# Attention's division moved behind attention, and ten expert conversions moved with it, in a hybrid decoder layer on eight cores

## The reference, cut to what matters

```python
# branch A, for each of 16 heads of 64: three (window, dilation) patterns, merged by their softmax denominators
num = sum(w * o for w, o in zip(weights, outs))
y_att = merge_heads(num / sum(weights)) @ w_att
# branch B: retention in chunks of 128, 4 heads, per-head norm, silu gate
y_ret = (merge_heads(rmsnorm(retention(q, k, v), g_ret)) * silu(gr)) @ w_ret
# merge
x = x + (sigmoid(ga + ba) * y_att + sigmoid(gb + bb) * y_ret) @ w_out
# then x = x + experts(rmsnorm(x)): 32 experts, top-2 inside the top-1 group of 8
```

## Time and profile before

| | us |
|---|---|
| median of three runs (1596.06 to 1598.11) | 1596.18 |
| the profiled execution | 1601.79 |
| its span on the slowest core, core 1 | 1597.6 |
| spans of the eight cores | 1574.9 to 1597.6 |
| TensorE busy | 1370.9 (86%) |
| VectorE, ScalarE, GpSimd busy | 763.3, 695.2, 762.8 |
| moved by DMA | 267.03 MB |

### The profile page before, as it was taken

The page is one execution under the profiler, slowest core; times in us unless marked ns, Lnnn a source line. Parts: engine busy times, 40 slices in busy tenths (PEclk is TensorE's granted clock), DMA queues, the critical chain, the costliest instruction groups (busy, mean ns, idle before and its releaser), DMA issues.

```text
span 1597.6 us, 29878 instructions; the slowest of 8 cores (1574.9 to 1597.6 us)
## 1 busy us (share of the span) xinstructions
PE 1370.9 (86%) x10037; PEld 789.1 (49%) x10037; DVE 763.3 (48%) x1239; ACT 695.2 (44%) x1191; POOL 762.8 (48%) x874
## 2 busy tenths in 40 slices
PE   4899998888879999999999899999999736565675
PEld 2344547776744444444444444444445435454563
DVE  3787774766656556555656411111354652211122
ACT  3576668887853444434443411111233542222232
POOL 1379981333236657666756312221225645543453
PEclk9999999998999999999999999999999957887888
DMA  9747866786765769999994399875964785999985
GB/s 221 215 92 131 165 155 177 163 188 139 179 138 89 118 101 131 125 131 146 122 137 123 61 289 166 131 125 129 244 220 154 228 286 153 275 254 251 281 162 91
DMA packets 105502, 267.03 MB, mean 167 GB/s; under 512 B 43352, under 2 KB 65368, under 8 KB 98818
## 3 DMA queue, kind: packets, MB, share of 16 engines
q0 software_dynamic: 29280, 124.30, 49.7%
q1 hardware_dynamic: 76066, 140.76, 28.4%
HBM read 285.71 MB, written 116.65 MB: 252 GB/s over the span
## 4 chain that ended last, share of the span: by engine, by line
PE 69%; DMA 13%; DVE 5%; issue 4%; ACT 4%; POOL 2%; SPq 1%; another core or an unknown queue 0%; DVEq 0%; POOLq 0%; ACTq 0%
PE ps L169 69%; DMA arena<-xn,idx 8%; DMA zret<-arena 5%; DVE arena L169 4%; ACT arena L169 3%; POOL arena L169 2%; DMA cfs_sb<-cfs 1%; DVE arena L167 1%; SPq L169 1%; DMA vp<-arena 0%; DVEq L156 0%; DVE logit L169 0%; ACT L169 0%; POOLq L176 0%
## 5 line engine op out<-in xcount | busy, mean ns | idle before, releaser
L169 PE MATMUL ps<-arena 128*128 128x512 bf16 (+5 forms) x8208 | 1275.5, 313 | 78.5 <-ACT arena L169 32.5
L169 PEld LDWEIGHTS ps<-arena 128*128 128x128 bf16 (+1 forms) x8208 | 679.0, 102 | 587.1 <-issue 122.4
L169 ACT ACTIVATE arena<-ps 128x512 bf16<-128x512 f32 (+5 forms) x600 | 422.5, 719 | 450.6 <-PE ps L169 412.2
L169 POOL TENSOR_TENSOR arena<-arena 128x512 bf16<-128x512 f32 (+4 forms) x274 | 347.7, 1278 | 297.9 <-DVE arena L169 244.7
L169 DVE TENSOR_TENSOR arena<-ps,arena 128x512 f32<-128x512 f32 (+4 forms) x420 | 235.3, 572 | 347.0 <-ACT arena L169 159.8
L169 PE MATMUL ps<-cbs_sb,arena 128*128 128x128 bf16 x1408 | 131.1, 232 | 107.3 <-DMA arena<-xn,idx 69.7
L169 DVE SCALAR_TENSOR_TENSOR arena<-arena,ps 128x512 f32<-128x512 f32 x176 | 115.5, 683 | 192.3 <-PE ps L169 190.7
L169 PEld LDWEIGHTS ps<-cbs_sb,arena 128*128 128x128 bf16 x1408 | 100.7, 104 | 176.2 <-issue 147.8
L169 ACT ACTIVATE arena<-arena 128x8 f32<-128x8 f32 (+5 forms) x225 | 148.6, 665 | 59.0 <-DVE arena L169 29.1
L169 DVE TENSOR_TENSOR arena<-arena 128x1024 bf16<-128x1024 bf16 (+9 forms) x176 | 130.7, 750 | 75.7 <-ACT arena L169 68.7
L169 POOL DMA_INDIRECT out<-arena,idx x48 | 76.3, 1590 | 126.5 <-ACT arena L169 66.6
(11 more groups left out here) (60 smaller groups left out, 339.9 us busy)
## 6 DMA issues: line engine op xcount, KB each, us to landing
wb<-wexp POOLq DMA_DIRECT2D x60, 768.0 KB, 13.8
arena<-wb SPq DMA_DIRECT2D x30, 1536.0 KB, 15.4
arena<-x SPq DMA_DIRECT2D x32, 512.0 KB, 7.8
arena<-vx POOLq DMA_DIRECT2D x12, 768.0 KB, 5.1
arena<-wri POOLq DMA_DIRECT2D x8, 1024.0 KB, 23.1
zret<-arena SPq DMA_DIRECT2D x16, 512.0 KB, 19.8
arena<-zret SPq DMA_DIRECT2D x4, 2048.0 KB, 17.2
out<-arena SPq DMA_DIRECT2D x16, 512.0 KB, 9.8
```

Of the source, the lines that this page charges most:

```text
L169: ins = getattr(engobj, meth)(*a, **kw)
```

## The change

Five edits, made together:

1. **The division leaves attention.** `den_shift`, `den_act` and `z_out` are gone. After its last copy each head stores its numerators (64 rows of 2048 float32) and one row of denominators to DRAM (`head_out`). In step 1 of retention one VectorE reciprocal works on all 16 x 2048 denominators as a 128x256 tile (`den_rec`), which goes back to DRAM.
2. **The division is done in 32 pieces of 128x512**, one for each pair and group c. `div_load` loads numerators (128 rows of 2 KB) and the reciprocals spread over 64 partitions for each of the two heads (128 rows of 2 KB), and `div_mul` multiplies on VectorE into `za[c]`. Groups 0 and 1 are done in steps 51 to 61 of retention with four buffers, groups 2 and 3 in the first merge pass with three, every two and then every four matmul pieces. The load of a buffer is issued after the multiply that frees it. `za` is no longer loaded.
3. **The bias** is kept for two items of a head (3 and 5) and becomes a VectorE mask for two (2 and 4).
4. **Conversions**: 11 in QKV, 6 in attention, 26 in retention, 10 in the first merge pass, 7 in the second. They go in the order in which the experts are used, in groups of four, and a half is written as six pieces a row where it was two. Merge weight blocks are written as four and six pieces a row where they were one and two.
5. **The first merge pass** does its first nine units as (0,0), (1,0), (0,1), (1,1), (2,0), (2,1), (0,2), (1,2), (2,2). `zr[0]` is loaded in step 62 of retention, not 57. Several tiles get other addresses.

```diff
-        CVE = [e for e in range(NE) if e not in EORD[:NDIR]]
-        NCV = 8
+        CVE = EORD[NDIR:]
+        NCV = 4
...
-                i = e // (NE // NCV)
+                i = u // 2 // NCV
...
-                p.dma(wb_d[e][:, cs].rearrange("p (a b) -> p a b", a=2), wexp_d[e][:, cs].rearrange("p (a b) -> p a b", a=2),
+                p.dma(wb_d[e][:, cs].rearrange("p (a b) -> p a b", a=6), wexp_d[e][:, cs].rearrange("p (a b) -> p a b", a=6),
...
-            if 24 <= ucount[0] < 96 and ucount[0] % 9 == 0:
+            if 24 <= ucount[0] < 96 and ucount[0] % 9 == 0 or ucount[0] in (30, 33, 40):
                 convert(1)
...
+        def head_out(pr, e):
+            h, r0, d0, i = 2 * pr + e, e * 64, 64 - e * 64, (2 * pr + e) % NXO
+            p.dma(num_d[h * 64:(h + 1) * 64, :], xo[i][r0:r0 + 64, :], reads=Rxo[i], writes=[Rnum[h]], semkey=("zatt", i))
+            p.dma(den_d[h:h + 1, :], xo[i][d0:d0 + 1, :], reads=Rxo[i], writes=[Rdend[h]], semkey=("xin", i))
...
-                todo.setdefault(g + 1, []).append(lambda: (osb_copy(pr, eh, 3), den_shift(pr, eh, 1)))
-                if eh == 1:
-                    for hf in range(2):
-                        for lag, f in ((1, lambda hf=hf: den_act(pr, hf, AF.Ln, 1.0)), (3, lambda hf=hf: den_act(pr, hf, AF.Exp, -1.0)),
-                                       (5, lambda hf=hf: z_out(pr, hf) if pr < 7 else deferred.append(lambda: z_out(pr, hf)))):
-                            todo.setdefault(g + lag + 4 * hf, []).append(f)
+                todo.setdefault(g + 1, []).append(lambda: (osb_copy(pr, eh, 3), head_out(pr, eh)))
...
-            queue.append((pr, eh, n_, S_item(pr, eh, kind, j, n_ in (2, 3, 4, 5))))
+            queue.append((pr, eh, n_, S_item(pr, eh, kind, j, n_ in (3, 5))))
...
+        def den_rec():
+            OP("dve", "reciprocal", out=dall, in_=dall, reads=[Rdall], writes=[Rdall])
+            p.dma(rden_d.rearrange("h (a b) -> (h a) b", a=8), dall, reads=[Rdall], writes=[Rrden], semkey="gqkb")
...
+        def div_load(c):
+            pr, i = dv[0] % 8, dv[0] % len(nb)
+            dv[0] += 1
+            cs = slice(c * 512, c * 512 + 512)
+            p.dma(nb[i], num_d[pr * 128:(pr + 1) * 128, cs], reads=Rnum[2 * pr:2 * pr + 2], writes=[Rnb[i]], semkey=("vp", i))
+            for e in range(2):
+                p.dma(rb[i][e * 64:(e + 1) * 64, :], rden_d[2 * pr + e, cs].partition_broadcast(64), reads=[Rrden], writes=[Rrb[i][e]],
+                      semkey=(("zero", i // 2, i % 2), ("qz", i // 2, i % 2, False))[e])
+
+        def div_mul(c):
+            pr, i = dv[1] % 8, dv[1] % len(nb)
+            dv[1] += 1
+            OP("dve", "tensor_tensor", out=za[c][:, pr, :], in0=nb[i], in1=rb[i], op=ALU.mult, reads=[Rnb[i]] + Rrb[i],
+               writes=[Rza[c][pr]])
...
-            load_cast(d[:, 0:2048], wm_d[fc][:, 0:2048], 1, Rwm[i][0], ("wm", i, 0))
-            load_cast(d[:, 2048:5120], wm_d[fc][:, 2048:5120], 2, Rwm[i][1], ("wm", i, 1))
+            load_cast(d[:, 0:2048], wm_d[fc][:, 0:2048], 4, Rwm[i][0], ("wm", i, 0))
+            load_cast(d[:, 2048:5120], wm_d[fc][:, 2048:5120], 6, Rwm[i][1], ("wm", i, 1))
...
-                if deferred:
-                    deferred.pop(0)()
+                if s_ == 1:
+                    den_rec()
+                if s_ == 48:
+                    za_alloc(0, 168)
+                    za_alloc(1, 192)
+                    div_bufs((176, 180, 184, 188))
+                    for u_ in range(4):
+                        div_load(0)
+                if 51 <= s_ < 62:
+                    for _ in range(1 + (s_ % 2 == 1 and s_ < 60)):
+                        div_mul(dv[1] // 8)
+                        if dv[0] < 16:
+                            div_load(dv[0] // 8)
                 pending = pending[take:]
-                if s_ % 4 != 1 and s_ < 48:
+                if s_ < 48 and s_ * 26 // 48 < (s_ + 1) * 26 // 48:
                     convert(1)
...
-        order = [(0, 0), (1, 0), (0, 1), (1, 1), (0, 2), (1, 2)]
-        order += [(fc, c) for fc in range(2, 8) for c in range(LC)]
+        order = [(0, 0), (1, 0), (0, 1), (1, 1), (2, 0), (2, 1), (0, 2), (1, 2), (2, 2)]
+        order += [(fc, c) for fc in range(3, 8) for c in range(LC)]
...
                 piece(fc, c, n, 4 * (un % 2), 0, "pool")
+                pi = 5 * un + n
+                if pi >= 10 and dv[1] < 16 and (pi % 2 == 0 if dv[1] < 8 else pi % 4 == 0):
+                    div_mul(2 + dv[1] // 8)
+                    if dv[0] < 16:
+                        div_load(2 + dv[0] // 8)
...
+            if s_ < 7:
+                convert(1)
```

More of the change, by code:

```diff
@@ L447, in build_nc @@
         EORD = [(q % 4) * 8 + q // 4 for q in range(NE)]
-        CVE = [e for e in range(NE) if e not in EORD[:NDIR]]
-        NCV = 8
-        Rcv = [[] for i in range(NCV)]
+        CVE = EORD[NDIR:]
+        NCV = 4
+        Rcv = [[] for i in range(-(-len(CVE) // NCV))]
         conv_at = [0]
@@ L763, in build_nc @@
         xo = [alloc([128, S], F32, Rxo[i]) for i in range(NXO)]
[L764 to L767, removed]
+        Rnum = [p.res(f"num{h}") for h in range(16)]
+        Rdend = [p.res(f"dend{h}") for h in range(16)]
         slot = [0]
@@ L1021, in build_nc, with div_bufs @@
         assert apos[0] <= 167 * KB, apos[0]
+        areset(92 * KB, 96 * KB)
+        Rdall = p.res("dall")
+        dall = alloc([128, 256], F32, [Rdall])
+        Rrden = p.res("rden")
+        p.dma(dall, den_d.rearrange("h (a b) -> (h a) b", a=8), reads=Rdend, writes=[Rdall], semkey="rawtab")
+        Rnb = [p.res(f"nb{i}") for i in range(4)]
+        Rrb = [[p.res(f"rb{i}_{e}") for e in range(2)] for i in range(4)]
+        nb, rb, dv = [], [], [0, 0]
+        def den_rec():
+            OP("dve", "reciprocal", out=dall, in_=dall, reads=[Rdall], writes=[Rdall])
+            p.dma(rden_d.rearrange("h (a b) -> (h a) b", a=8), dall, reads=[Rdall], writes=[Rrden], semkey="gqkb")
+        def div_bufs(at):
+            assert dv[0] == dv[1]
+            del nb[:], rb[:]
+            for i, k in enumerate(at):
+                areset(k * KB)
+                nb.append(alloc([128, 512], F32, [Rnb[i]]))
+                rb.append(alloc([128, 512], F32, Rrb[i]))
+            dv[:] = [0, 0]
+        def div_load(c):
[11 more added lines that the diff above has]
+               writes=[Rza[c][pr]])
         INNER = ps[:, 3, 0:128]
@@ L1143, in build_nc @@
         za, zr = {}, {}
-        Rza = [[p.res(f"za{c}")] for c in range(NG)]
+        Rza = [[p.res(f"za{c}_{k}") for k in range(8)] for c in range(NG)]
         Rzr = [[p.res(f"zr{c}")] for c in range(NG)]
@@ L1196, in build_nc @@
                     load_wm(1)
-                if s_ == 57:
-                    areset(168 * KB)
-                    z_alloc(0)
-                    load_za(0)
+                if s_ == 62:
+                    assert dv[1] == 16
+                    zr_alloc(0, 176)
                     load_zr(0)
-        areset(56 * KB)
-        for c in (1, 2):
-            z_alloc(c)
-            load_za(c)
-            load_zr(c)
+        zr_alloc(1, 64)
+        load_zr(1)
+        div_bufs((56, 60, 124))
+        for u_ in range(3):
+            div_load(2)
+        za_alloc(2, 80)
+        zr_alloc(2, 88)
+        load_zr(2)
+        za_alloc(3, 152)
+        areset(104 * KB)
         wm.append(alloc([128, 40, 128], BF16, Rwm[2]))
@@ L1210, in build_nc @@
         RmT = [[p.res(f"mT{c}_{k}") for k in range(8)] for c in range(NG)]
-        mT = [alloc([128, 8, 512], BF16, RmT[c]) for c in range(NG)]
+        mT = [alloc([128, 8, 512], BF16, RmT[c]) for c in range(NG - 1)]
+        areset(160 * KB)
         Rwo = [p.res(f"wo{i}") for i in range(2)]
         wo = [alloc([128, 8, 512], BF16, [Rwo[0]])]
-        areset(192 * KB)
+        areset(116 * KB, 124 * KB)
         wo.append(alloc([128, 8, 512], BF16, [Rwo[1]]))
@@ L1292, in build_nc @@
                     xres_load(t)
-        assert conv_at[0] == 2 * len(CVE), conv_at
         WXPOS = (0, 12, 24, 36, 104, 136, 48, 148, 160, 60, 116, 72)
@@ L1308, in load_wx @@
                 return
-            p.dma(wx[i], wb_d[e], reads=Rcv[e // (NE // NCV)], writes=[Rwx[i]], semkey=("wx", i))
+            assert conv_at[0] >= min(2 * len(CVE), 2 * NCV * ((q - NDIR) // NCV + 1))
+            p.dma(wx[i], wb_d[e], reads=Rcv[(q - NDIR) // NCV], writes=[Rwx[i]], semkey=("wx", i))
         for q in range(NDIR):
@@ L1667, in build_nc @@
                 load_wx(q)
-        assert not fill
+        assert not fill and conv_at[0] == 2 * len(CVE)
         route_exp(*pend)
```

38 lines of the change are left out of this document (12 added, 26 removed).

## The result

The change made the kernel slower: 1.040 times the kernel before, 95% interval 1.035 to 1.046. Undisturbed runs took 1661.47 and 1664.51 us, against 1596.06 to 1604.40 before; two more runs, in which the granted clock of one die's cores was 0.80 to 0.89, are left out. The forecast was 1571, in 1555 to 1590.

A forecast was written before the change was run, and what follows sets the result against it. TensorE was taken to bound the kernel nearly everywhere, with a real gap only in attention. Gains of 37 us less losses of 12.5 took the profiled 1601.79 to 1577, or 1571 for the median; range 1555 to 1590.

The forecast's parts named there:

- 26 + 8 - 2 = 32: Attention: gain 26 us from denominator work leaving, 8 from masks on VectorE, loss 2 from larger stores.
- the control: Attention: a head without denominator work took 11.32 us against 13.2 with it, pricing that work at 3.8 us a pair.
- more bytes out: Attention: float32 numerators, 512 KB a head instead of 256, plus denominator rows put q0 behind; loss 0 to 10, taken 2.
- QKV, 0.5: QKV: three more conversions cost GpSimd about 0.6 us an issue; loss 0 to 2 us, taken 0.5.
- -2: Retention: ten fewer conversions relieve q0 and end VectorE's store waits; gain 0 to 6 us, taken 2.
- +1: Late retention: work queues behind a division multiply whose load is late, so TensorE waits; loss 0 to 8 us, taken 1.
- First merge pass, 3: First merge pass: late weight block 3 and the multiplies' loads; loss 0 to 20 us, taken 3.
- rival C: First merge pass: multiplies' loads starve beside full q0, VectorE blocks PSUM banks, TensorE loses 76 us; 1644 in all; chance 0.06.
- block-3 wait: First merge pass: weight block 3, issued later, leaves 13 us before unit 9 uses it; stall of 0 to 9 us.
- Second merge pass, 6, bounded at 16: Second merge pass: seven added conversions make input rows late, holding residual and TensorE; loss 0 to 16 us, taken 6.
- Finer pieces: Conversions and merge weight blocks: cutting rows finer makes no smaller packets, so it was costed at nothing.
- B: Merge passes: second stalls in full and block 3 too, 16 + 9 us where 9 was taken; 1587; chance 0.16.

The follow-up runs named there:

- 4 copies: Changed kernel with conversions issued where before, numerators stored piece by piece, 4 stored copies of each reciprocal row, each read 16 times: 0.988 of the kernel before.

## Why the prediction was wrong

- **Attention: right in mechanism, too large:** 21 us on the slowest core, 22 in the medians, where 26 + 8 - 2 = 32 was the sum. Undisturbed heads lost what the control said (13.2 to 11.3, then 10.6 to 11.1 with the mask), and the mask is worth its 8. The term that was mis-sized is the denominators' 26 less 2 for "more bytes out", which measured 14. On the slowest core instruction waits rose from 6.7 to 16.9 us, which takes back 10 of the 34; on core 5 they rose only from 3.6 to 5.6, and attention there became 28.6 us shorter (206.3 to 177.7). What makes instructions late was not isolated.
- **QKV, 0.5: the step that failed** is the cost of a moved conversion. I priced GpSimd's issue and no transfer. Its DMA delays SP's 384-byte v rows (a store of them landed after 52 us, after 13 at most before); three more conversions cost 14 to 18 us.
- **Retention: -2 right, +1 wrong.** By step 48 the stage is 4.4 us ahead, pair 7's 1.9 included; the division in its last steps then costs 11.3, because its loads are slow. With 4 copies retention takes 451, as before.
- **First merge pass, 3: the step that failed most** is rejecting rival C by "SP's loads passed at several times that rate when q0 was not full". That rate came from stores and loads of distinct rows. The division's loads read one row 64 times, a form that no row of before shows, and they are slow with q0 empty. Rival C's picture (VectorE at a multiply, finished banks behind it) is what the trace shows, but its cause, turns beside q0, is not what decided: other rows cure the stage with q0 as it was. Its 76 us came out as 42 here, with 11 more in retention, and that its 1644 lies near the measured time is luck, since it holds neither QKV's 16 us nor 20 of the second pass's 26. The block-3 wait that I did foresee is there, 12.7 us, but it too goes with the loads.
- **Second merge pass, 6, bounded at 16:** 23 to 26. The mechanism was named (late input rows hold the residual and TensorE), the bound was too low: it let the excess of 16 us pass once, while one load of input rows took 46 us from issue to landing, with SP's queue at a third of the engines.
- **Finer pieces: right.** GpSimd's queue has 29,280 packets before and after.
- **The range** left out the cause that decided, since rival C had 0.06 and B's cap was worked out from shares. The signs that I had named for C and B, VectorE waiting for a load in the first merge pass and TensorE idle behind the residual, both came.

## What to carry to other kernels

Price a moved transfer by what queues beside it, not by its issue: name every small store whose buffer an engine needs again. Never price a load by the rate of another access pattern; a broadcast from DRAM over many partitions is a form of its own and wants its own row, or a few stored copies. Here 4 copies, one store of 512 KB, turned the 2.7% of loss that was left with the conversions put back into a gain of 0.4%, and with numerators stored close into one of 1.2%.

## What the runs showed of the hardware

- **One DRAM row read for 64 partitions** is slow: loads of which such rows are half took 6.1 to 6.2 us of all engines a megabyte, against 3.1 with four stored copies of the row, and under load a mean of 219 to 248 ns a 2 KB row against 119. That it is many engines at one row at once is the likely reading, not shown.
- **The outermost dimension sets how many engines serve a transfer**: with 4 outermost, 4 of 16 engines were busy, for stores from 4 partitions and for loads from a source of [4, 16, 512] alike; reordered to 16, the same bytes took 14 us less in the first merge pass. The Trainium skill (DMA: Bandwidth & Descriptors, Rules for kernel authors) says that a short outermost dimension confines a transfer to at most as many engines; these traces agree.
- **A reciprocal of 128x512** on VectorE took 3.35 us, almost five times the 0.69 us of a multiply of that size.
